# A two-block transformer kernel: splits, compressed keys, a value matmul and key scores in another place

## The reference

```python
def compress(kv, pe, w1, w2):
    ...
    hid = jax.nn.silu(jnp.einsum('bnlgd,lde->bnge', blocks, w1))
    return jnp.einsum('bnge,ef->bngf', hid, w2)
...
    q = (zc @ peer_wq).astype(jnp.float32).reshape(PEER_CHUNK, PEER_HEADS, 2, PEER_HALF)
    s1 = jnp.einsum('chd,hkd->chk', q[:, :, 0], k1)
    s2 = jnp.einsum('chd,hkd->chk', q[:, :, 1], k2)
    v1, i1 = lax.top_k(s1, PEER_TOPK)
    v2, i2 = lax.top_k(s2, PEER_TOPK)
    ...
    u = jnp.take(peer_u, expert, axis=0)
    act = jax.nn.gelu(jnp.einsum('chkd,cd->chk', u, zc))
    v = jnp.take(peer_v, expert, axis=0)
```

## Time and profile before

| | |
|---|---|
| median of 3 runs | 2532.5 us (2532.36 to 2532.8) |
| profiled execution | 2528.8 us, its span 2527.0 us |
| PE busy | 2170.8 us, 86% |
| DVE busy | 1508.9 us, 60% |
| ACT, POOL busy | 698.6 and 710.4 us, 28% each |
| DMA | 755.63 MB |
| median time of a gather of `peer_v` from issue to landing | 27.9 us |

### The profile page before, as it was taken

The page is one execution under the profiler, slowest core; times in us unless marked ns, Lnnn a source line. Parts: engine busy times, 40 slices in busy tenths (PEclk is TensorE's granted clock), DMA queues, the critical chain, the costliest instruction groups (busy, mean ns, idle before and its releaser), DMA issues.

```text
span 2527.0 us, 32248 instructions
## 1 busy us (share of the span) xinstructions
PE 2170.8 (86%) x12044; PEld 1607.8 (64%) x12044; DVE 1508.9 (60%) x2144; ACT 698.6 (28%) x1163; POOL 710.4 (28%) x649
## 2 busy tenths in 40 slices
PE   8999999999999999999987678766877668776786
PEld 8999999999999999999943233322333223332232
DVE  5445555555556576867975556555565555655545
ACT  5444544554344344635311001000010000100001
POOL 3000000000000422221475344443444434443341
PEclk9999999999999999999989899888988899888998
DMA  9634444465657545475999999999999999999997
GB/s 272 198 109 148 144 148 140 144 200 167 220 170 246 163 154 163 139 223 160 349 415 422 421 422 421 422 422 421 422 421 422 421 421 422 422 422 422 422 422 299
DMA packets 281389, 755.63 MB, mean 299 GB/s; under 512 B 12033, under 2 KB 213201, under 8 KB 214609
## 3 DMA queue, kind: packets, MB, share of 16 engines
q0 software_dynamic: 74432, 539.07, 51.6%
q1 hardware_dynamic: 206624, 215.28, 27.3%
q10 hardware_dynamic: 240, 0.07, 0.0%
HBM read 752.26 MB, written 2.10 MB: 299 GB/s over the span
## 4 chain that ended last, share of the span: by engine, by line
PE 50%; DMA 35%; DVE 7%; issue 3%; POOL 3%; ACT 1%; ACTq 0%; POOLq 0%; DVEq 0%
PE PS L1752 39%; DMA RZ<-in_peer_u,idxu 18%; DMA RAW<-in_peer_u,idxu 17%; PE PS L2045 6%; DVE RZ L1600 2%; POOL EX L618 2%; DVE RAW L1600 2%; DVE WL L1089 1%; PE PS L1895 1%; DMA EX<-in_peer_v,idxv 1%; PE PS L1815 1%; PE PS L1873 1%; POOL RAW L618 1%; PE PS L1883 0%; PE PS L1972 0%
## 5 line engine op out<-in xcount | busy, mean ns | idle before, releaser
L2045 PE MATMUL PS<-EX,RK 128*128 128x512 f32 x1968 | 906.8, 615 | 314.6 <-ACT RK L1054 188.1
L2045 PEld LDWEIGHTS PS<-EX,RK 128*128 128x128 f32 x1968 | 376.9, 197 | 843.7 <-issue 716.6
L1752 PE MATMUL PS<-XH,WH 128*128 128x256 f32 x2896 | 799.7, 285 | 4.2 <-ACT XH L853 1.2
L1752 PE MATMUL PS<-XH,WL 128*128 128x256 f32 x2896 | 793.9, 283 | 0.0
L1752 PE MATMUL PS<-XL,WH 128*128 128x256 f32 x2896 | 723.7, 283 | 3.1 <-DVE XL L1099 3.1
L1089 DVE TENSOR_TENSOR WL<-RAW,WH 128x1024 fp32r<-128x1024 f32 x380 | 474.5, 1260 | 385.0 <-ACT WH L707 382.0
L1752 PEld LDWEIGHTS PS<-XH,WH 128*128 128x128 f32 x2896 | 555.5, 192 | 7.7 <-issue 5.8
L1752 PEld LDWEIGHTS PS<-XH,WL 128*128 128x128 f32 x2896 | 555.5, 192 | 0.0
L707 ACT ACTIVATE WH<-RAW 128x1024 fp32r<-128x1024 f32 x380 | 400.0, 1059 | 552.4 <-PE PS L1752 543.8
L1752 PEld LDWEIGHTS PS<-XL,WH 128*128 128x128 f32 x2896 | 513.4, 192 | 3.8 <-DVE XL L1099 3.5
L1600 DVE CUSTOM_DVE_ANT_0 RZ<-RZ 128x2048 f32<-128x2048 f32 x126 | 288.8, 2292 | 250.0 <-DMA RZ<-in_peer_u,idxu 249.6
(11 more groups left out here) (343 smaller groups left out, 1354.3 us busy)
## 6 DMA issues: line engine op xcount, KB each, us to landing
RAW<-in_w_in SPq DMA_DIRECT2D x110, 1024.0 KB, 5.2
RAW<-in_w_out SPq DMA_DIRECT2D x32, 1024.0 KB, 5.6
RAW<-in_w_ple_gate SPq DMA_DIRECT2D x16, 1024.0 KB, 5.7
RAW<-in_peer_wq SPq DMA_DIRECT2D x16, 1024.0 KB, 5.7
RAW<-in_w_up_a SPq DMA_DIRECT2D x8, 1024.0 KB, 5.6
RAW<-in_w_up_b SPq DMA_DIRECT2D x8, 1024.0 KB, 5.6
EX<-in_peer_v,idxv POOLq DMA_INDIRECT x252, 27.9
RZ<-in_x SPq DMA_DIRECT2D x2, 1024.0 KB, 6.2
```

The source lines that it names most:

```text
L1752: ins = mm(o[:, t, :], left, right, start=(begins and k == t == m == 0), stop=(ends and k == QUARTER_KT - 1 and m == len(pairs) - 1), skip ...
L2045: ins = mm(bank(4 * (1 - hf) + c), left, right[:, 512 * c:512 * (c + 1)], start=False, stop=True, skip_group_check=True)
```

## The change

`last_panel` now takes each chunk of the operand right behind the same quarter of the weights, on ACT and on DVE. The small products of the compressed keys move into the middle of panel 5 of kv, and DVE's copies between its quarters 1 and 2. The value matmul of the compressed keys reads all 128 rows, of which POOL has cleared those behind the 16th. The scores of head 0 stay where they are; those of heads 1 to 3 move from before quarter 2 to before quarter 3 of panels 2 to 4, and those of heads 4 to 7 behind the loop.

```diff
+SCORED = 4
...
             g.wait_ge(S["xt_done"], 4)
+            line.do(g.memset(pts[:, 768:1024], 0.0))
...
             def last_panel(section, j, i, chunk, evac=None):
-                split_next(section, j, i, quarters=range(3))
+                for q in range(3):
+                    split_next(section, j, i, quarters=(q,))
+                    chunk(q)
                 done(section, j, i)
-                chunk(0)
                 if evac is not None:
                     evac()
-                chunk(1)
-                chunk(2)
                 split_next(section, j, i, quarters=(3,))
                 chunk(3)
...
             for j in range(8):
                 if j < 7:
-                    split_next("wq", j, quarters=(0, 1))
-                if j:
+                    split_next("wq", j, quarters=(0, 1) if j == 1 else (0, 1, 2))
+                if 1 <= j <= SCORED:
                     key_scores(j - 1)
                 if j < 7:
-                    split_next("wq", j, quarters=(2, 3))
+                    split_next("wq", j, quarters=(2, 3) if j == 1 else (3,))
...
-            key_scores(7)
+            for h in range(SCORED, PEER_HEADS):
+                key_scores(h)
...
             def last_panel(section, j, i, chunk, evac=None):
-                split_next(section, j, i, quarters=range(3))
-                chunk(0)
+                for q in range(3):
+                    split_next(section, j, i, quarters=(q,))
+                    chunk(q)
                 if evac is not None:
                     evac()
-                chunk(1)
-                chunk(2)
...
             for j in range(6):
-                split_next("kv", j)
+                split_next("kv", j, quarters=(0, 1) if j == 5 else range(QUARTERS))
...
                                     ALU.mult).then_inc(S["vall_ready"], 1)
+                    split_next("kv", j, quarters=(2, 3))
...
                     if q == 2 and middle is not None:
                         middle()
+                    if q == 3 and third is not None:
+                        third()
...
+            def compressed():
+                pe.wait_ge(S["hid_ready"], 3)
+                mm(bank(4)[:, 0:2 * NC_BLOCKS], w2bd[:, 0, :], hid[:, 0, :], start=True, stop=True).then_inc(S["kc_done"], 1)
...
             for j in range(6):
-                product("kv", j)
+                product("kv", j, middle=compressed if j == 5 else None)
...
-                    mm(pO, vcur[0:NCP, 4, cols], pts[0:NCP, 768:1024], start=False, stop=(par == 1), skip_group_check=True)\
+                    mm(pO, vcur[:, 4, cols], pts[:, 768:1024], start=False, stop=(par == 1), skip_group_check=True)\
...
             for j in range(8):
-                product("wq", j, operand="z3" if j == 0 else None, middle=(lambda: key_scores(j - 1)) if j else None)
+                product("wq", j, operand="z3" if j == 0 else None, middle=(lambda: key_scores(0)) if j == 1 else None,
+                        third=(lambda: key_scores(j - 1)) if 2 <= j <= SCORED else None)
...
-            key_scores(7)
+            for h in range(SCORED, PEER_HEADS):
+                key_scores(h)
```

More of the change, by code:

```diff
@@ L1723, in _, with product @@
             pe.sem_inc(S["pv_done"], AHEAD)
-            def product(section, j, i=0, operand=None, tiles=2, outs=None, middle=None, second=None, by_tokens=False):
+            def product(section, j, i=0, operand=None, tiles=2, outs=None, middle=None, second=None, third=None, by_tokens=False):
                 b = bank_of(section, j)
@@ L1798, in _ @@
             product("gl", 0, tiles=1)
+            def compressed():
+                pe.wait_ge(S["hid_ready"], 3)
+                mm(bank(4)[:, 0:2 * NC_BLOCKS], w2bd[:, 0, :], hid[:, 0, :], start=True, stop=True).then_inc(S["kc_done"], 1)
+                for t in range(2):
+                    ins = mm(bank(5)[0:NC_BLOCKS, t * P:(t + 1) * P], hid[:, 1, t * NC_BLOCKS:(t + 1) * NC_BLOCKS], w2bd[:, 1, :], start=True, stop=True)
+                ins.then_inc(S["kc_done"], 1)
             for j in range(6):
-                product("kv", j)
+                product("kv", j, middle=compressed if j == 5 else None)
                 if j == 0:
@@ L1823, in _ @@
                     ins.then_inc(S["small_t"], 1)
[L1824 to L1830, removed]
             def values(typ, which):
```

## The result

The changed kernel takes 2513.31 us (median of 6 runs, 2512.9 to 2513.59), the kernel before 2532.19 in the same comparison (6 runs, 2531.14 to 2532.8). The ratio is 0.9926, 95% interval 0.9913 to 0.9939, which is 15.4 to 22.0 us: 18.9 us less, where I had forecast 16.3. The profiled executions tell another number: 2528.8 us before, 2512.9 after, 15.9 us less. That is what the experiments had to explain. One execution of the kernel before, further on, took 2625.45 us at a granted clock of 0.816, a slower state, and is not counted.

What follows compares the result with a forecast made beforehand. TensorE was taken to set the pace until about 1206 us, then DMA's expert-row gathers. 6.4 + 1.05 + 5.8 + 3.0 = 16.3 us off 2532.5 gave 2516.2 us; own range 2514 to 2519, wide range 2513.5 to 2522.5.

Steps and rivals of the forecast that it cites:

- the wide one: The wider predicted range for the whole kernel, covering the forecast and two rivals: 2513.5 to 2522.5 us.
- Term 1: At five borders, operand splits between the weight quarters remove TensorE's waits and gaps: 6.4 us, bounds 5.3 and 6.7.
- The rule of starts: Counting TensorE's gaps from matmul start to start: a gap costs its wait plus 0.16 to 0.26 us.
- The fifth border: The border from up to out: no gap to win, because TensorE turns x there meanwhile.
- Term 2: In panel 5 of kv, moving the compressed keys removes TensorE's wait: 1.05 us, bounds 0.6 and 1.5.
- The new wait at the key copies: In kv, TensorE would stand about 0.4 us before the second pair of key copies.
- Term 3: In the loop over the groups, 128 rows in place of 16 at 16 matmuls: 5.8 us, bounds 0 and 5.8.
- Rival A: At the compressed keys' value matmul, full height inherits the narrow one's gaps, so 128 rows gain nothing: 2522.0 us, chance 0.11.
- Rival C: The first index list doesn't move with TensorE, since DVE or weight loads pace it: no change, 2532.5 us, chance 0.04.
- Term 4: Moving key scores in the wq loop puts TensorE ahead, filling idle DMA at 1245 to 1270 us: 3.0 us, bounds 0 and 3.5.
- Rival B: The wq loop gives nothing because POOL's issues stay the limit: 2519.2 us or up to 2 more, chance 0.14.
- Rival D: Scores behind the loop delay the token-order matmuls, POOL's gather stands and DMA runs dry: 2533 us and more, chance 0.04.

Runs made afterwards that it cites:

- before again: The kernel before, unchanged, run once more with a second profile: 2532.27 us.
- borders alone: The kernel before with only the operand chunks put between the weight quarters at the five borders: 2523.79 us against 2530.95.
- the kernel with the two places mended: The kernel before with the compressed keys moved inside panel 5 of kv and the new order at the ple to in2 border only: 2525.38 us against 2532.26.
- the scores alone: The kernel before with only the key scores moved (heads 1 to 3 a quarter later, 4 to 7 behind the loop): 2529.56 us against 2530.95.
- the late heads alone: The changed kernel, but scores of heads 1 to 3 in the middle of the product as before; heads 4 to 7 stay behind the loop: 2513.14 us.
- seven scores in the loop: The changed kernel, but scores of heads 1 to 6 a quarter later and only head 7 behind the loop: 2513.32 us.
- The filled wait: The changed kernel with the old order at ple to in2 and 18 extra unread matmuls issued in its wait: 2515.74 us against 2532.26 before.

## Why the prediction was wrong, and what in it was right

The step that failed is the last one of the sum: "the median of the runs stands 3.7 above it, and from 2532.5 I forecast 2516.2 us". I took the distance between the profiled execution and the median for something that the change leaves alone. After the change it was 0.4 us (2513.31 less 2512.9), so 3.3 of the 3.7 were gone; the traces moved by 15.9 for the sum's 16.3, and 3.3 - 0.4 is the 2.9 by which the forecast was off. Most of the distance was the change's to remove. The first profile happened to have neither fall of the clock, which is bad luck in the choice of a baseline: of 86 further executions of that kernel 5 come within 1 us of it. How far the forecast stood outside its range is luck too: the second series of the changed kernel, 2513.88, lies inside the wide one. Of the profiles with the old wait at "kv" 2 of 6 show the fall (before again, borders alone), of those with the old wait at "in2" (unfilled) 5 of 7; of those where the wait was removed, shortened or filled none does, at "kv" 10, at "in2" 9. For "in2" that is clear; at "kv" counts of 2 in 6 and 0 in 10 would come out so by chance in one case of eight, and the cause rests on the groups of the executions as well. Besides, the stretch behind the first gather in that profile, 1320.42 us, was the shortest of seven without the score move (up to 1322.18, mean 1321.3). At those rates the falls cost 1.69 x 2/6 + 1.49 x 5/7 = 1.6 us on average, which with the 0.9 of the gathers makes 2.5 of the 3.7; the kernel with the two places mended speaks for more, 3.1, and so do the groups, where about half of the executions have the time of both falls. That share is an estimate from times; only profiled executions show a fall.

**Term 1, borders:** 6.4 predicted, 6.86 found (1.46 + 1.03 + 2.88 + 1.49), 0.2 above my upper bound. The rule of starts was right for three borders: with 0.19 us a gap they come to 1.43, 0.99 and 2.79, and 1.46, 1.03 and 2.88 were found. Most of the rest lies at the start of "wq", where 0.85 and two gaps of 0.19 make 1.23 and 1.49 was found. The fifth border gave nothing, as said.

**Term 2, kv:** 1.05 predicted, 0.87 found. The new wait at the key copies is 0.5 us, not 0.4.

**Term 3, 128 rows:** 5.8 predicted, 5.60 found, in every trace that has it. Rival A is refuted: full height costs no more than its neighbours. Of the two rules that I had set beside the rows, the one in the Trainium skill's "TensorE: Matmul & The Clock Gate", Why this matters for your kernels, by which K = 32 takes the time of K = 128, doesn't hold in this place: 0.20 us of the 0.34 that are gone lay in the narrow pair's own step, 0.09 in the step before it and 0.05 in the one behind. For a matmul that stands alone no run shows it. The Trainium skill's "TensorEngine Tiling (Array Packing)", Key Properties, which has the array drain at a change of mode, agrees with these runs, though they don't show that a drain is what took the time.

**Terms 1 to 3 together:** 13.25 predicted, 13.33 found, and the first gather at 1194.97 for 1195.1. Rival C fell with it.

**Term 4, scores:** 3.0 predicted. Behind the first gather the seven profiles with the whole move of the scores have 1317.6 to 1318.1 us, mean 1317.9, the seven without it 1320.4 to 1322.2, mean 1321.3: 3.4 us. By medians it is 1.7 (2515.55 less 2513.88), and 1.4 for the scores alone, which isn't clear of noise; so the size lies between 1.7 and 3.4 and stays open. Rival B is refuted: the five executions without the move (2515.04 and more) all lie above the eleven of the changed kernel (2514.39 at most). That DMA fills its idle time is shown by the stretch from 40 to 60 us behind the first gather; the reason was half right. I had wanted PE's in-loop waits away and the late heads out of the loop, but by medians either is enough. In the profiles the late heads alone close the idle time (406 GB/s) and seven scores in the loop close it only in part (375). What limits it after that wasn't tried.

**Rival D** didn't come: POOL's wait for the token-order matmuls became 1.15 us and DMA stood at 419 GB/s and more from 1255 us on, while PE waited.

## What to carry to other kernels

Before the terms of a sum are laid on a profiled execution, look at the spread of the runs: if it is as wide as a term of the sum, compare the granted clock by windows in two profiles of the same kernel, and ask whether the change touches the places where they differ. A short wait of TensorE ahead of dense work may cost its own length and, in some executions, 1.4 to 1.7 us again; removing it narrowed the spread here (6.5 to 2.5 us with two places mended) as well as lowering the median. And where the wait can't be removed, extra matmuls that nobody reads can be cheaper than standing still: 18 of them gave 2.2 us here.

## What the runs showed of the hardware

A wait of 2.25 us, in a stretch of otherwise dense matmuls, was enough for TensorE's granted clock to fall, in five profiles of seven: a 256-column matmul then followed another by 0.21 us in place of 0.12, which is the lower of its levels, 1.2 for 2.4 GHz, and it stayed there until 908.70. Behind the wait of 1.39 us at the end of "kv", with small matmuls and transposes before and behind it, the clock fell in two profiles of six; the waits of 1.2 us (merge to up) and 0.8 (out to ple) didn't in any of the seven profiles that have them, nor that of 1.1 (border of "y") in any of sixteen. The same kernel has the fall in one execution and not in the next. The Trainium skill's "TensorE: Matmul & The Clock Gate", Part 1, names the two levels and says that activity releases the throttle, and that the number of slow matmuls varies from run to run. The filled wait agrees with the first: with activity in it there was no fall, and 1.49 us were won. The page tells the second of the start of a kernel; here it is the falls in its middle that come in one execution and not in another. The second surprise is the price of a 16-row matmul among full-height ones: 0.35 us more for each (5.60 us over 16), beside the 0.43 us that its two passes take at full height.
